# The four retention products of a head, side by side over the blocks of tokens instead of one behind the other

## The reference, cut to what matters

```python
scores = jnp.einsum('bhid,bhjd->bhij', qc, kc) * intra_decay
o = jnp.einsum('bhij,bhje->bhie', scores, vc)      # plus the state of earlier chunks
...
mu = jnp.mean(o, axis=-1, keepdims=True)
var = jnp.mean(jnp.square(o - mu), axis=-1, keepdims=True)
o = (o - mu) * lax.rsqrt(var + EPS)
o = merge_heads(o).astype(h.dtype) * jax.nn.silu(g)
y = o @ ret_w_out[i]
```

## Time and profile before

| | us |
|---|---|
| median of 3 runs | 1860.28 (1859.43 to 1861.7) |
| the profiled execution, its own time | 1861.27 |
| its span, first to last instruction | 1859.5 |
| PE busy | 1833.6 (99%) |
| DVE busy | 1397.1 (75%) |
| ACT busy | 930.3 (50%) |

### The profile page before, as it was taken

The page is one execution under the profiler, slowest core; times in us unless marked ns, Lnnn a source line. Parts: engine busy times, 40 slices in busy tenths (PEclk is TensorE's granted clock), DMA queues, the critical chain, the costliest instruction groups (busy, mean ns, idle before and its releaser), DMA issues. The chain is left out here.

```text
span 1859.5 us, 28152 instructions
## 1 busy us (share of the span) xinstructions
PE 1833.6 (99%) x11311; PEld 1640.3 (88%) x11311; DVE 1397.1 (75%) x1912; ACT 930.3 (50%) x1274; POOL 81.6 (4%) x109
## 2 busy tenths in 40 slices
PE   9999999999999999999999899999999999999997
PEld 7998998888888988989998799988888888888886
DVE  8875887888778878856888877766777776666666
ACT  6652664435355535634653454455446644444445
POOL 0000000120000000000000010000000000000000
PEclk9999999999999999999999999999999999999999
DMA  6744762462417526654743589631331222222213
GB/s 213 184 125 123 197 172 100 176 151 70 118 46 208 148 93 168 166 161 122 195 117 109 167 239 260 224 144 68 114 136 48 91 86 73 91 70 88 90 68 91
DMA packets 61026, 246.87 MB, mean 133 GB/s; under 512 B 6912, under 2 KB 9504, under 8 KB 50160
## 3 DMA queue, kind: packets, MB, share of 16 engines
q1 hardware_dynamic: 46448, 201.35, 31.9%
q0 software_dynamic: 14032, 43.38, 12.3%
q10 hardware_dynamic: 432, 0.56, 0.1%
HBM read 224.81 MB, written 14.16 MB: 129 GB/s over the span
## 5 line engine op out<-in xcount | busy, mean ns | idle before, releaser
L1452 DVE TENSOR_TENSOR w_lo<-raw,w_hi 128x2048 fp32r<-128x2048 f32 (+1 forms) x106 | 239.0, 2254 | 48.8 <-ACT w_hi L734 48.6
L734 ACT ACTIVATE w_hi<-raw 128x2048 fp32r<-128x2048 f32 (+1 forms) x106 | 199.3, 1880 | 75.2 <-PE acc L2562 61.6
L2560 PE MATMUL acc<-x_hi,w_hi 128*128 128x512 f32 x488 | 193.3, 396 | 1.0 <-DVE x_lo L1515 0.7
L2566 PE MATMUL acc<-xt_hi,w_hi 128*128 128x256 f32 x684 | 192.2, 281 | 1.7 <-ACT tmp L833 1.7
L2567 PE MATMUL acc<-xt_lo,w_hi 128*128 128x256 f32 x684 | 191.7, 280 | 0.0
L2568 PE MATMUL acc<-xt_hi,w_lo 128*128 128x256 f32 x684 | 191.7, 280 | 0.0
L2562 PE MATMUL acc<-x_hi,w_lo 128*128 128x512 f32 x488 | 190.3, 390 | 0.0
L2561 PE MATMUL acc<-x_lo,w_hi 128*128 128x512 f32 x488 | 190.1, 390 | 0.0
L833 ACT ACTIVATE tmp<-acc 128x256 f32<-128x256 f32 x228 | 86.8, 381 | 125.8 <-PE acc L2568 116.6
L2561 PE MATMUL acc<-g_lo,w_hi 128*128 128x512 f32 x352 | 137.0, 389 | 0.0
L2560 PE MATMUL acc<-g_hi,w_hi 128*128 128x512 f32 x352 | 137.0, 389 | 0.0
(11 more groups left out here) (506 smaller groups left out, 5125.3 us busy)
## 6 DMA issues: line engine op xcount, KB each, us to landing
raw<-in_ffn_down SPq DMA_DIRECT2D x32, 704.0 KB, 4.2
raw_c<-in_ffn_seven SPq DMA_DIRECT2D x37, 512.0 KB, 5.3
raw<-in_ffn_seven SPq DMA_DIRECT2D x33, 512.0 KB, 4.9
raw<-in_ffn_seven POOLq DMA_DIRECT2D x33, 512.0 KB, 7.3
raw<-in_ffn_seven SPq DMA_DIRECT2D x37, 256.0 KB, 4.4
kept<-unit_out SPq DMA_DIRECT2D x16, 512.0 KB, 6.4
raw<-in_ret_values SPq DMA_DIRECT2D x8, 1024.0 KB, 4.8
raw<-in_ret_out SPq DMA_DIRECT2D x8, 1024.0 KB, 6.9
```

The costliest lines, as they stand in the source:

```text
L734: nc.scalar.activation(w_hi[:, slot, at:at + cols], raw[:, slot, 0:cols], ACT.Copy).then_inc(w_hi_ready, 1)
L1452: tt(w_lo[:, slot, at:at + cols], raw[:, slot, 0:cols], w_hi[:, slot, at:at + cols].bitcast(F32), ALU.subtract).then_inc(w_ready, 1)
L2560: mm(dst, still[0], move[0], start=first, stop=False)
L2566: mm(dst, still[0], move[0], start=first, stop=False, skip_group_check=True)
```

## The change

The loops over the products c and the blocks m change places. All four banks are taken first; then block m's part is done for all four products before block m+1. The waits for block m stand once ahead of block m, and each product's count-up of `att_full` stands at its last instruction, in the last block. The instructions of the section are the same 48 in another order. No other engine's program is changed.

```diff
                 ret_values(slab(), v_banks, 1)
-                for c in range(RET_VC):
-                    dst = side_bank()
-                    for m in range(TB):
-                        if c == 0:
-                            pe.wait_ge(op_ready, op.at(m + 1))
-                            pe.wait_ge(acc_free, u.at(BANKS - TB + m + 1))
-                        cols = slice(TRI_AT[m], TRI_AT[m] + TRI[m])
-                        ins = passes(dst[:, P * m:], (rv_hi[:, m, P * c:P * c + P], rv_lo[:, m, P * c:P * c + P]),
+                sums = [side_bank() for c in range(RET_VC)]
+                for m in range(TB):
+                    pe.wait_ge(op_ready, op.at(m + 1))
+                    pe.wait_ge(acc_free, u.at(BANKS - TB + m + 1))
+                    cols = slice(TRI_AT[m], TRI_AT[m] + TRI[m])
+                    for c in range(RET_VC):
+                        ins = passes(sums[c][:, P * m:], (rv_hi[:, m, P * c:P * c + P], rv_lo[:, m, P * c:P * c + P]),
                                      (rs_hi[:, cols], rs_lo[:, cols]), m == 0, m == TB - 1)
-                    ins.then_inc(att_full, 1)
+                        if m == TB - 1:
+                            ins.then_inc(att_full, 1)
                 op.next(TB)
                 sq.next()
```

## The result

The changed kernel takes 1873.88 us in the median of 4 runs (1870.54 to 1875.24). The kernel before took 1860.37 beside it (4 runs, 1859.43 to 1861.7). The ratio is 1.0069, with a 95% interval of 1.0052 to 1.0087. It is slower by 13.5 us. The forecast said slower, by 6.4, in a range that ended at 1871.5, so the sign was right, the size was half of what came, and the time lies outside the range.

The account below looks back on a forecast made before the run. PE was taken to bound the kernel, busy 99% of the span. Per head -1.04 for the old wait and +2.65 for the new gave +1.6, four heads +6.4, so 1866.7 us from 1860.28; range 1864.0 to 1871.5.

Parts of the forecast that it names:

- The wait that goes: PE's wait for `rv_lo` ahead of block 3 in product 0 goes in full: -1.04 us a head, -4.2 in all.
- The 48 instructions: The four products' section on PE keeps its length, 7.62 us a head; change taken as 0, bounds -0.7 and +0.1.
- The chain and the new wait: Product 0's square, gate, addition and low part end late; PE waits 2.65 us a head before the output product.
- Chunks 1 to 3, the norm, the second slab: Later places in the output product and the next weight split: delayed work is ready in time, no new PE waits.
- The sum without the clock: Per head -1.04 + 2.65 = +1.6 us, for four heads +6.4 us.
- The clock: Rival, chance 0.33: PE's clock falls to half in the new wait; most for one or two heads, 1868 to 1873.
- The price of a fall: Each clock fall slows up to 6.8 us of 512-wide products, losing up to 3.4 us, or 1.5 if shorter.
- the two falls: Clock falls before the change: in PE's 5.4 us wait, and at the kernel's end 3.1 us after the last issue.
- The hidden chain: Rival, chance 0.04: ACT and DVE start product 0 early enough, only the gain of 4 x 1.04 is left, 1856.1.
- the four banks: Rival, chance 0.05: PE waits at the banks being taken, a fraction of a microsecond a head, 1868 or so.

Follow-up runs that it names:

- e2: Against the kernel before: two banks open at a time, products 0 and 1 side by side, then 2 and 3, in every head; 1855.79 us, ratio 0.9979.
- e3: Changed kernel with DVE's low part of chunk 0 moved ahead of the gate of product 1 and the first addition of squares; 1868.71 us, ratio 1.0045.
- e1: Changed kernel with ten 512-wide filler products a head on PE, between the 48 products and the wait for chunk 0; 1866.66 us, ratio 1.0036.
- e8: Kernel before, old product order, with PE waiting ahead of output chunk 0 for the low parts of chunks 0 to 2; 1876.87 us, ratio 1.0094.
- e4: Kernel before with the loops swapped in the last head only, the first three heads unchanged; 1863.52 us, ratio 1.0017.
- e5: Changed kernel with three 512-wide filler products a head on PE before the wait for chunk 0; 1867.74 us, ratio 1.0039.
- e6: Changed kernel with six 512-wide filler products a head on PE before the wait for chunk 0; 1865.5 us, ratio 1.0033.

## Why the prediction was right or wrong

**The wait that goes.** Right. Block 3's wait has vanished from the waits of PE, and e2, which adds none in its place, gained 4.5 us where 4.2 were given.

**The 48 instructions.** Right. The section takes 1229.34 + 0.11 - 1221.91 = 7.54 us; the forecast had 7.62. Going round four banks cost nothing that can be seen.

**The chain and the new wait.** Right to 0.01 us at each step named above, and PE's two starts are 2.77 us apart where 2.65 + 0.11 were forecast. The queue order on DVE was worth reading: e3 shows that 0.5 us of the wait was the gate and the addition that stood ahead of the low part.

**Chunks 1 to 3, the norm, the second slab.** Right: the waits' view has nothing at these places.

**The sum without the clock.** Right: +6.2 in the trace, +6.35 in e1, +6.4 forecast.

**The clock.** This is the step that failed: the sum put it at nothing, and it cost 7.2 to 8.4 us. The prediction gave a fall 0.33 and "most of it for one or two heads", and let the range end at 1871.5. The clock fell in all four heads. The price of a fall, 1.5 to 3.4 us, was right (8.4 us for four in the trace; 7.2 between the changed kernel and e1). What was wrong was the use of the two falls that the trace of before showed. I read the shorter one, 3.1 us after an issue, as if it were a limit, and set "2.8 is below the shortest case shown" against the rival. But those two stops were long ones, 5.4 us and the end of the kernel. They show that such a stop is enough, and nothing about what a shorter one does. All waits of PE in the kernel before that were longer than the 0.8 us of the earlier trace rows, from the view of its waits:

```profile
PE acc L2566 <- DVE w_lo L1559: 5.4, 1, 5.4
...
PE acc L2566 <- ACT tmp L833: 1.7, 2, 0.9
PE att L2711 <- DVE tmp L1745: 1.5, 1, 1.5
```

The 1.5 us is the wait for the first product of the kernel, with none ahead of it. So behind products the longest wait that left the clock alone was 0.9 us and the shortest with a fall 5.4, and 2.65 lay where nothing had been seen. That gave no ground for making the fall the less likely case, and since the four heads wait alike, it had to be priced for all four. With 1.5 to 3.4 us for each the forecast would have been 1873 to 1880. That all four did fall is in part luck: in e3 and e8 one of four waits, as long as the other three, left the clock at 1.00.

Waits of 2.0 to 2.7 us lowered the clock in 11 heads of 13, and one of 1.6 us in 1 of 4. The Trainium skill, "TensorE: Matmul & The Clock Gate", section "Why this matters for your kernels", which advises against gaps of more than about 3 us, is too wide for this kernel; the measurement decides.

**The other rivals.** The hidden chain did not happen: product 0 is complete 1.0 us before product 3 (1228.34 and 1229.34 in the trace), as the loops say. No wait at the four banks appeared.

## What to carry to other kernels

Opening all banks at once makes the first result as late as the last; its consumer's chain is then bare. Open just as many as it takes to cover the wait at hand: two here, which cover 2.54 us with 3.1 and leave 3.9 for the chain. When a forecast adds a wait to a queue that has none, ask first what lies between the longest wait that left the clock alone and the shortest that lowered it; if the new one falls in between, price it both ways for every place at which it stands, and let the range hold both.

## What the runs showed of the hardware that was not expected

How long after PE's last product the granted clock falls is not one figure. In the changed kernel four waits of the same length lie behind the same products. The stretch around each fall, in windows, and the second head's last product before the wait and first behind it:

```profile
1231.00:1232.00 1.00, 0.00 (x0) 0.00 (x0) 0.96 (x3) 1.00 (x3) 0.00 (x0) 0.93 0.00 0
1293.00:1294.00 1.00, 1.00 (x5) 0.77 (x4) 0.96 (x3) 0.26 (x1) 0.00 (x0) 0.65 0.07 16
1351.00:1352.00 1.00, 0.00 (x0) 0.00 (x0) 0.96 (x2) 1.00 (x3) 0.00 (x0) 0.66 0.00 0
1412.50:1413.50 1.00, 0.00 (x0) 0.00 (x0) 0.96 (x3) 1.00 (x3) 0.00 (x0) 0.63 0.00 0
```

```profile
1289.37 0.28 PE L2562 MATMUL att<-rs_hi,rv_lo 128*128 128x128 f32 x1
...
1292.14 0.47 PE L2560 MATMUL acc<-w_hi,rg_hi 128*128 128x512 f32 x1 [2.49 <-DVE rg_lo L1476]
```

A mean of 0.63 over the last microsecond puts the fall at 1412.76. Worked out so, the four falls came 2.5, 3.9, 1.8 and 1.9 us after the last issue, where the trace of before had 4.2 and 3.1. In the second head the clock fell 1.15 us after PE had gone on. So the 3.1 us of before was no limit, and ending a wait ahead of such a figure does not make it safe. The length of a wait does not settle whether the clock falls either: of e8's four alike, the first did not lower it. What else decides it stays open.

How long the stretch at 0.50 lasts goes with when it begins. The two falls of the changed kernel that came before PE went on by 0.8 us or more lasted about 6.8 us, as did the one of the kernel before, which came 1.6 us ahead. The two that came 0.3 us before or later lasted 3.4, and so did all eight falls of e3, e4, e5 and e8, none of which came more than 0.3 us ahead. From run to run the loss differs: the four runs of the changed kernel lie 4.7 us apart, and the fastest has the highest mean clock, 0.994 against 0.990 and 0.991. Only one of the four was profiled, so whether its falls were fewer or shorter can't be told. The ten runs of e2, where nothing waits, lie 3.2 us apart, seven of them within 0.8. Why the length takes these two values was not tested.

Instructions that do nothing useful can pay: e1's forty extra products made the changed kernel 7.2 us faster, by holding the clock up in a wait. e6's twenty-four did as well. Taking the wait away, as e2 does, is worth more.
